# A decoder step: sample attention in two groups of four batches, on four column quarters of the array

## The reference

```python
def mla_attend(q_lat, q_rope, ckv, krope, q_pos, k_pos):    # q_lat (B,T,H,C), ckv (B,S,C)
    ...
    s = (jnp.einsum('bthc,bsc->bhts', ql, ckv) + jnp.einsum('bthr,bsr->bhts', qr, krope)).astype(jnp.float32) * SOFTMAX_SCALE
    s = jnp.where(k_pos[None, :] <= qp[:, None], s, -jnp.inf)
    p = jax.nn.softmax(s, axis=-1).astype(ckv.dtype)
    return jnp.einsum('bhts,bsc->bthc', p, ckv)
...
q_nope, q_rope = q[..., :NOPE_DIM], rope(q[..., NOPE_DIM:], pos)
q_lat = jnp.einsum('bthn,chn->bthc', q_nope, w_uk)
...
past_ckv = cache_ckv[page_table].reshape(bs, n_pages * PAGE_SIZE, KV_LORA)       # 8 x 1024 x 256
past_krope = cache_krope[page_table].reshape(bs, n_pages * PAGE_SIZE, ROPE_DIM)  # 8 x 1024 x 64
```

## Time and profile before

| | us |
|---|---|
| median of three runs | 1940.32 |
| the profiled execution | 1941.86 |
| its span, first to last instruction | 1940.2 |
| prompt attention, from its first transpose | 546.2 to 623.5 |
| sample attention | 623.5 to 787.0 |
| value and output products, router, tables | 787.0 to 885.5 |
| expert loop | 885.5 to 1923 |

### The profile page before, as it was taken

One profiled execution on the slowest core, in us unless ns is written; L12 is line 12 of the kernel. 1 busy time (PEld: TensorE's weight loads), 2 busy tenths in 40 slices (PEclk: granted clock), 3 DMA queues, 4 the chain that ended last, 5 costly groups with the idle time before them and its releaser, 6 DMA issues.

```text
span 1940.2 us, 23808 instructions
## 1 busy us (share of the span) xinstructions
PE 1807.1 (93%) x8518; PEld 1390.7 (72%) x8518; DVE 1234.8 (64%) x1350; ACT 912.4 (47%) x813; POOL 39.5 (2%) x77
## 2 busy tenths in 40 slices
PE   7999999997977888968999999999999999999996
PEld 4566799995555333756877878878778788787784
DVE  2134354443443222257889888898898888988987
ACT  2013234330111111214676666766766667667665
POOL 0000000000000120000000000000000000000000
PEclk9998999998966888968999999999999999999998
DMA  9102233462310120024998989989989898898893
GB/s 403 79 23 109 93 134 128 146 236 107 135 52 0 44 65 28 14 109 163 348 356 330 346 332 358 345 319 347 348 330 354 330 359 342 318 348 344 340 347 138
DMA packets 67413, 438.68 MB, mean 226 GB/s; under 512 B 8656, under 2 KB 17104, under 8 KB 18976
## 3 DMA queue, kind: packets, MB, share of 16 engines
q1 hardware_dynamic: 64128, 432.17, 58.6%
q0 software_dynamic: 2640, 5.52, 0.8%
q10 hardware_dynamic: 592, 0.26, 0.0%
HBM read 434.00 MB, written 3.93 MB: 226 GB/s over the span
## 4 chain that ended last, share of the span: by engine, by line
PE 88%; DVE 5%; issue 2%; ACT 2%; SPq 1%; DMA 1%; DVEq 0%; ACTq 0%
PE bank L374 16%; PE bank L376 16%; PE bank L375 16%; PE bank L370 11%; PE wide L376 3%; PE wide L374 3%; PE wide L375 2%; PE bank L723 2%; PE wide L706 2%; PE bank L764 2%; PE wide L833 1%; PE bank L667 1%; PE wide L383 1%; PE wide L863 1%; PE bank L693 1%
## 5 line engine op out<-in xcount | busy, mean ns | idle before, releaser
L926 DVE TENSOR_TENSOR wpart<-mring,wpart 128x2048 fp32r<-128x2048 f32 x339 | 775.1, 2288 | 139.6 <-ACT wpart L1627 138.8
L1627 ACT ACTIVATE wpart<-mring 128x2048 fp32r<-128x2048 f32 x336 | 643.4, 1917 | 257.3 <-PE bank L376 144.6
L374 PE MATMUL bank<-wpart,xgp 128*128 128x512 f32 x896 | 359.6, 401 | 1.5 <-DVE cols L1371 1.5
L375 PE MATMUL bank<-wpart,xgp 128*128 128x512 f32 x896 | 354.3, 395 | 0.0
L376 PE MATMUL bank<-wpart,xgp 128*128 128x512 f32 x896 | 354.3, 395 | 0.0
L374 PEld LDWEIGHTS bank<-wpart,xgp 128*128 128x128 f32 x896 | 168.6, 188 | 41.3 <-issue 1.9
L376 PEld LDWEIGHTS bank<-wpart,xgp 128*128 128x128 f32 x896 | 168.4, 188 | 41.0
L375 PEld LDWEIGHTS bank<-wpart,xgp 128*128 128x128 f32 x896 | 168.7, 188 | 38.3
L374 PE MATMUL bank<-ffparts,wpart 128*128 128x288 f32 x528 | 157.5, 298 | 5.2 <-DVE ffparts L926 4.2
L376 PE MATMUL bank<-ffparts,wpart 128*128 128x288 f32 x528 | 157.1, 298 | 0.0
L375 PE MATMUL bank<-ffparts,wpart 128*128 128x288 f32 x528 | 154.5, 293 | 0.0
(11 more groups left out here) (339 smaller groups left out, 2070.9 us busy)
## 6 DMA issues: line engine op xcount, KB each, us to landing
mring<-in_w_moe SPq DMA_DIRECT2D x339, 1024.0 KB, 4.9
ring<-in_c_dd SPq DMA_DIRECT2D x8, 1408.0 KB, 6.9
ring<-in_c_gd SPq DMA_DIRECT2D x5, 2048.0 KB, 8.0
ring<-in_c_ud SPq DMA_DIRECT2D x5, 2048.0 KB, 8.6
arena<-in_cache_ckv SPq DMA_DIRECT2D x48, 128.0 KB, 2.0
ring<-in_c_v SPq DMA_DIRECT2D x2, 2048.0 KB, 21.6
ring<-in_c_o SPq DMA_DIRECT2D x2, 2048.0 KB, 30.2
ring<-in_c_out SPq DMA_DIRECT2D x2, 2048.0 KB, 24.5
```

The lines of the kernel that those rows point to most:

```text
L374: pe.matmul(o, a[0], b[0], start=start, stop=False)
L375: pe.matmul(o, a[1], b[0], start=False, stop=False)
L926: return v.tensor_tensor(dst, src, high.bitcast(F32), ALU.subtract)
L1627: a.activation(wpart[:, stage(h), 0, :], mring[:, place(h % IH), :], ACT.Copy).then_inc(S["hi_ready"], 1)
```

## The change

Sample attention runs in two groups of four batches. The four batches of a group stand side by side: batch b of the group writes its scores and its weighted sum to partitions 32b to 32b+31, that is, from the b-th quarter of the array's columns. So one mask, one maximum, one exponential and one normalisation serve four batches, with 128 partitions.

- The host lays the cached keys out turned, 128 partitions x 384 numbers per page (two blocks of compressed keys, one of rotary keys filled up with zeros to 128 rows), so the kernel turns no page. It lays out w_uk turned too, so `ukT` is the chunk itself and the 16 transposes and 4 copies go. `krT` and `qrs` get 128 rows, of which 64 are zero (two memsets).
- A page is loaded twice: as keys by SP (192 KB, into slots 4 to 6 of the ring) and as values by POOL (128 KB, into the arena). A group is 32 pages on either queue. Group 0 is issued when the dense SwiGLU has ended; group 1's keys when group 0's scores are done, its values when group 0's weighted sums are done. SP's pages stand on its queue between the weight chunks.
- Group 0 runs ahead of prompt attention, group 1 behind it. `p_scores(0)` and `p_scores(1)` stand between group 0's turning of the probabilities and its weighted sums.
- `uq1`, `uv`, `wo0` move to slots 1, 2, 3. The seven first halves of expert 0 wait for `uq1`, `uq1`, `uv`, `uv`, `wo0`, `wo1`, `wo1`. The first split into `wpart` waits for group 1's scores.

```diff
+            def group_scores(x):
+                pe.wait_ge(keys_full[x], 16 * GB * NPG)
+                for part in range(2):
+                    for k in range(CT + 1):
+                        for b in range(GB):
+                            q = qls[:, k, GB * x + b, :] if k < CT else qrs[:, GB * x + b, :]
+                            pe.matmul(wide[b * TS:(b + 1) * TS, part * 512:(part + 1) * 512], q,
+                                      keys_[:, b, part * 4:part * 4 + 4, k * P:(k + 1) * P], start=(k == 0), stop=(k == CT))
+                for k in range(CT + 1):
+                    q = qls[:, k, GB * x:GB * (x + 1), :] if k < CT else qrs[:, GB * x:GB * (x + 1), :]
+                    ins = pe.matmul(wide[:, PAST:PAST + TS], q, ckvT[:, k, TP:T] if k < CT else krT[:, TP:T],
+                                    start=(k == 0), stop=(k == CT))
+                ins.then_inc(S["gs_full"], 1)
+            def group_turn(x):
+                pe.wait_ge(S["gp_exp"], x + 1)
+                for g in range(NPG):
+                    pe.transpose(bank[g // 4][:, (g % 4) * P:(g % 4 + 1) * P], prob[:, g * P:(g + 1) * P], ident)
+                pe.transpose(bank[2][0:TS, 0:P], prob[:, PAST:PAST + TS], ident).then_inc(S["gt_full"], 1)
+            def group_attend(x):
+                pe.wait_ge(S["gt_ready"], 2 * (x + 1))
+                pe.wait_ge(vals_full[x], 16 * GB * NPG)
+                for g in range(NPG):
+                    for b in range(GB):
+                        pe.matmul(bank[3][b * TS:(b + 1) * TS, 0:CKV], PTg[:, g * P + b * TS:g * P + (b + 1) * TS],
+                                  vals[:, b, g, :], start=(g == 0), stop=False)
+                pe.matmul(bank[3][:, 0:CKV], PTg[0:TS, NPG * P:(NPG + 1) * P], ctok[0:TS, 2, 0:CKV], start=False,
+                          stop=True).then_inc(S["gav_full"], 1)
+            def group_back(x):
+                pe.wait_ge(S["gos_ready"], x + 1)
+                for k in range(CT):
+                    ins = pe.transpose(bank[4][:, k * P:(k + 1) * P], osb[:, k * P:(k + 1) * P], ident)
+                ins.then_inc(S["gol_full"], 1)
+            group_scores(0)
+            group_turn(0)
             p_scores(0)
             p_scores(1)
+            group_attend(0)
+            group_back(0)
+            pe.wait_ge(S["gol_ready"], 1)
             for u in range(len(units)):
                 p_attend(u)
...
             pe.wait_ge(S["ol_ready"], NU)
-            cache_transposes(0)
-            for b in range(NB):
...
+            group_scores(1)
+            group_turn(1)
+            group_attend(1)
+            group_back(1)
+            pe.wait_ge(S["gol_ready"], 2)
             arrived("uv")
...
+            def group_max(x):
+                v.wait_ge(S["gs_full"], x + 1)
+                m = wide[:, PAST:PAST + TS]
+                link(v.tensor_tensor(m, m, c("smask")[:, x * TS:(x + 1) * TS], ALU.add))
+                link(v.reduce_max(cols[:, 2:3], wide[:, 0:PAST + TS], AX.X))
+                v.tensor_scalar(cols[:, 6 + x:7 + x], cols[:, 2:3], -SCALE, None, ALU.mult).then_inc(S["gm_ready"], 1)
...
+            def group_exp(x):
+                a.wait_ge(S["gm_ready"], x + 1)
+                a.activation(prob[:, :], wide[:, 0:PAST + TS], ACT.Exp, bias=cols[:, 6 + x:7 + x], scale=SCALE,
+                             accum_out=cols[:, (10, 3)[x]:(11, 4)[x]]).then_inc(S["gp_exp"], 1)
+                a.wait_ge(S["gt_full"], x + 1)
+                a.activation(PTg[:, 4 * P:NPG * P], bank[1][:, :], ACT.Copy).then_inc(S["gt_ready"], 1)
...
-            for name in ("uq1", "uv", "wo0"):
-                a.wait_ge(*release[CH[name]])
+            a.wait_ge(S["gs_full"], 2)
...
+            sp.wait_ge(S["gd_full"], GD_CKV)
+            sp.wait_ge(S["ld_pages"], 16)
+            load_keys(0, (0, 1))
+            load_chunk("uq1")
+            load_keys(0, (2, 3))
+            load_chunk("uv")
+            load_chunk("wo1")
+            load_chunk("wo0")
+            sp.wait_ge(S["gs_full"], 1)
+            load_keys(1, range(GB))
```

More of the change, by code:

```diff
@@ L273, in build @@
         CH = {name: n for n, (name, _, _) in enumerate(CHUNKS)}
-        slot_of = [0, 1, 4, 5, 2, 3, 6] + [n % 4 for n in range(CH["uq0"] + 1 - SLOTS)] + [4, 5, 6, 0]
+        slot_of = [0, 1, 4, 5, 2, 3, 6] + [n % 4 for n in range(CH["uq0"] + 1 - SLOTS)] + [1, 2, 3, 0]
         arrive, slot_sum, behind = [], [0] * SLOTS, []
@@ L629, in latent_q @@
                     o = out_d()
-                    done_d(pe.matmul(o[:, 0:T], ukT[:, h, k * P:(k + 1) * P], qn[h % 2], start=True, stop=True))
+                    done_d(pe.matmul(o[:, 0:T], ukT[:, h, k * P:(k + 1) * P], qn[h % 2], start=True, stop=True),
+                           "uk" if h == H - 1 and k == CT - 1 else None)
+            arrived("uk")
+            ukT = wview("uk", H, CKV)
             ga_q = n_ga[0]
@@ L1702, in _ @@
             sp.dma_start(xT[:, :, :], i["x"].rearrange("p (c t) -> p c t", c=DC)).then_inc(S["ld_x"], 16)
-            def load_cache(b):
-                with sp.Fori(0, NPG) as j:
-                    page = sp.value_load(pages[0:1, bass.ds(j + b * NPG, 1)], min_val=0, max_val=i["cache_ckv"].shape[0] - 1)
-                    sp.dma_start(ctk[b % BUFS][:, bass.ds(j, 1), :],
-                                 i["cache_ckv"][bass.ds(page, 1), :, :].rearrange("g p c -> p g c")).then_inc(ck_full[b % BUFS], 16)
@@ L1710, in _, with load_keys @@
-            for n, (name, k, w) in enumerate(CHUNKS):
-                if name == "dd4":
-                    sp.wait_ge(S["gd_full"], GD_FFN + FT)
-                    sp.wait_ge(S["hp_lo"], FT)
-                    sp.wait_ge(S["stored"], 16 * STORES_A)
-                    sp.wait_ge(S["ld_pages"], 16)
-                    load_cache(0)
-                    load_cache(1)
-                if slot_of[n] >= 4 and n >= SLOTS:
-                    sp.wait_ge(S["gd_full"], GD_CKV)
-                elif n >= SLOTS:
+            def load_keys(x, batches):
+                for b in batches:
+                    with sp.Fori(0, NPG) as j:
+                        page = sp.value_load(pages[0:1, bass.ds(j + (GB * x + b) * NPG, 1)], min_val=0, max_val=i["cache_keys"].shape[0] - 1)
+                        sp.dma_start(keys_[:, b, bass.ds(j, 1), :],
+                                     i["cache_keys"][bass.ds(page, 1), :, :].rearrange("g p c -> p g c")).then_inc(keys_full[x], 16)
@@ L1743, in item_first @@
                     expert_half(e, h)
-            under = [CH[name] for name in ("dkv", "dkv", "dq", "dq", "uk", "wo1", "wo1")]
+            under = [CH[name] for name in ("uq1", "uq1", "uv", "uv", "wo0", "wo1", "wo1")]
             for h in range(HALVES):
-                if h == 5:
-                    for b in range(2, NB):
-                        if b == 2:
-                            sp.wait_ge(*release[CH["uq1"]])
-                        else:
-                            sp.wait_ge(S["av_full"], b - BUFS + 1)
-                        load_cache(b)
                 sp.wait_ge(*release[under[h]])
@@ L1804, in shape_constants @@
     }
-    x = np.arange((2 * NB - 1) * NS)
-    parts["smask"] = np.where((x[None, :] // NS == NB - 1) & (x[None, :] % NS <= r[:, None] % NS), 0.0, NEG)
+    own = r // TS
+    parts["smask"] = np.concatenate([np.where((t[None, :] // NS == GB * x + own[:, None]) & (t[None, :] % NS <= r[:, None] % NS),
+                                              0.0, NEG) for x in range(2)], axis=1)
     half = ROPE // 2
```

234 lines of the change are left out of this document (69 added, 165 removed).

## The result

The changed kernel takes 1770.76 us, the median of four runs (1764.88 to 1770.95); the kernel before, on the same chip, 1941.73. The ratio is 0.911, 95% interval [0.909, 0.914]. The forecast was 1814 us with a range of 1798 to 1841, so the change is faster as forecast and the time lies 27 us under the range. The profiled execution took 1770.8 us, with a span of 1769.1.

A forecast was written before the change was run, and what follows sets the result against it. PE was taken as the bound (88% of the chain). Terms +15.2 - 142.9 - 2.2 - 0.8 + 1.5 + 2 = -127.2 us took the profiled 1941.86 to 1814.7; forecast 1814 us, range 1798 to 1841.

The forecast's parts named there:

- Products on four quarters: Sample attention: products on all four column quarters run together; 5.1 us for a group's scores, 3.4 for its weighted sums.
- Group 0 and group 1: Sample attention: group 0 ahead of the prompt adds 15.2 us; group 1 behind it replaces the old stage, -142.9 us.
- possible addition: Group 0: if the stretch runs at half clock, its 14 us of PE work double, up to +14 more.
- w_uk and the pages of the SwiGLU: Ahead of attention: dropping the w_uk transposes gives -2.2 us, taking page loads out of the dense SwiGLU -0.8 us.
- Pages in their new places: Page loads for both groups: all hidden behind other work, with at least 30 us to spare.
- rival 4: Page loads: from 3.0 us a page PE waits; at 5.5 us a page the time is 1975 us; chance 0.03.
- The clock of the prompt: Prompt attention: stays mostly at half clock, its full-clock opening lost in part; +1.5 us.
- Rival 3: Prompt attention: denser products in front could keep full clock within it; down to -25 us, 1790; chance 0.05.
- The expert loop: Expert loop: the change leaves it alone, cost 0; length 1037.5 us within 3.

The follow-up runs named there:

- batch-outer kernel: The changed kernel with a group's score products in the order batch, row block, pass instead of row block, pass, batch; 1794.86 us.

## Why the prediction was wrong

**Products on four quarters: right.** The trace took 5.36 us for 48 score instructions where 5.1 and a drain were forecast, and 3.66 for 64 of the weighted sum against 3.4. The step from two halves in the earlier trace rows to four quarters was the risky one, taken without a row, and it held. The Trainium skill's strict order ("TensorE: Matmul & The Clock Gate", Part 3, The mechanism) would have made it 10.2 us; the trace disagrees. Its 3.07 for four row tiles (Measured speedup) would give 6.7 us; the trace disagrees with that too. The ratio 15.7 / 5.36 = 2.9 of the batch-outer kernel only looks like it, since that kernel has some overlap.

**Group 0 and group 1: right.** 20.9 us against 19.4 (of which the listed items make 18.9 and unlisted gaps 0.5) and 21.1 against 20.5. The 1.5 us in group 0 are about what the half clock from 550.6 to 554.1 costs (the kernel with seven products in that wait took 19.2 us), which the prediction had left out of the term and named as a possible addition. In group 1 two errors met: the scores took 6.6 us where 8 was taken, and 0.9 us of own keys were missing from the list; the other items came within 0.6 us.

**w_uk and the pages of the SwiGLU: half seen.** From the first `dq` product to the reciprocal the stretch is 2.4 us shorter (19.0 us, then 16.6), as forecast. The 0.8 us can't be seen: the profiled execution after was already 2 us late when the SwiGLU began (232.8 against 230.8), and the kernel before reaches the prompt's first score at anything from 538.0 to 546.4 in the profiles of its variants with the same program up to there. ACT's wait for the weight chunk is gone.

**Pages in their new places: right.** No PE wait for a page. That the prompt covers group 1's keys is shown by the kernel without that cover, which stands 37 us for them. The prediction's price for a lost cover, 1.44 us "twice 32 times" (92 us), was too high, since group 0's keys stayed covered, and the rest of group 0 stood beside the first 13 us of group 1's. Slow pages, rival 4, did not occur.

**The clock of the prompt: wrong, the first failed step.** "I take +1.5" came out as -23.4. The prediction read the half clock of the earlier trace rows as a property of the stage and shifted only its opening. The runs showed that the same units also run at full clock for 50 us: the clock fell at 612.1, where it had fallen at 548.2 before. Rival 3 had the result and nearly the size (down to -25), with a chance of 0.05. Its mechanism, denser products in front, is not what happened: in the changed kernel the clock had fallen in group 0 and risen again 8 us ahead of the first unit, and with denser products there (seven more in each group, then three and three more) the stage fell back to half clock. That group 0 ahead of the prompt makes the difference is shown by the kernel with the prompt first, where it is missing; what in it does so is open. What the units' own waits do is shown by two products in each, which kept the clock up in the kernel before.

The trace before could have warned: 61.6 of 77.3 us busy at half clock is at least 31 at full clock (37.7 in the trace after), so PE would no longer bound the stage and its length would be set by DVE and ACT. How long that chain takes, 54 us, only the traces after show.

**The expert loop: wrong, the second failed step.** The prediction said "the change leaves it alone" and "the loop's length 1037.5 us within 3". No instruction changed; 32 bytes of layout did, and the loop gained 21 us. The prediction put the loop at nothing and did not ask what lies behind the wider `smask` in memory. The runs showed 2.2% more products in the same time, 21.2 us.

The two are 24.9 and 21.2 us, 46 together; the other terms came out 2 us dearer than forecast, which leaves the 44 us between 1814.7 and 1770.8.

## What to carry to other kernels

When a change alters the size of any tensor, look at where the operands of the hottest products come to stand before and after, and try them 32 bytes higher or lower; judge it by the number of instructions in a window, since the busy share does not show it. A stage at half clock whose bounding engine would be another one at full clock may run at either level: try unread products in its short waits, and inside the stage first, since fills ahead of it helped in the kernel before and moved the fall into the stage in the changed one. When products go to different quarters of the array, let neighbours in the program alternate between them.

## What the runs showed of the hardware

- F32R products with a 128 x 128 stationary operand and 512 moving columns ran 2.2% slower with the stationary tensors 32 bytes above or below byte 212608 of a partition: 3518 in place of 3594 instructions in 800 us. One fast address and two slow ones, with the moving operand's tensor in one place, do not give the rule.
- Four column quarters gave the full factor four: 48 instructions of 512 columns in 5.36 us, when neighbours alternate; 15.7 us when they don't.
- A stage of units with a PE wait of about 1 us in each lost full clock in all fifteen profiles, at 0 to 10 us or at 50 us from its start, and took 76 us or more with an early fall, 54 with a late one. One kernel did both in different runs, to judge by their times (1754 to 1760 us and 1786 us; one of the latter has a trace). What decides between early and late was not settled. With two unread products in each unit it kept full clock to its end in four profiles of four, and none of the 17 runs of those kernels was longer by more than 8 us than its median.
